# A decode step on one core: the residual stream stored tile by tile, each after its last addition, in place of one store at the end

## The reference

```python
def swiglu(h, w_gu, w_down):
    gu = h @ w_gu
    return (jax.nn.silu(gu[..., :D_FF]) * gu[..., D_FF:]) @ w_down
...
        x = x + jnp.concatenate([mix, mem_o], axis=-1) @ prm['w_out'][l]
        x = x + swiglu(rmsnorm(x, prm['g_ffn'][l]), prm['w_gu'][l], prm['w_down'][l])
...
    s_win = jnp.concatenate([cache_win_kv, rows_s[2]], axis=1)[:, -wb:]
```

## Time and profile before

| what | value |
| --- | --- |
| median of 3 timed executions | 3421.77 us |
| lowest and highest of them | 3414.11 and 3422.32 us |
| the profiled execution's own time | 3419.85 us |
| span of its trace, from the first to the last instruction | 3418.1 us |
| mean granted TensorE clock over the span | 0.937 of full speed |

### The profile page before, as it was taken

How to read it: one execution, slowest core, us unless ns; L and a number is a source line. 1 busy time by engine, 2 the same in 40 slices (tenths; PEclk the granted TensorE clock), 3 DMA queues, 4 the chain that set the end, 5 groups by cost and what they waited for, 6 DMA issues and landing times.

```text
span 3418.1 us, 49546 instructions
## 1 busy us (share of the span) xinstructions
PE 3093.7 (91%) x20055; PEld 2893.8 (85%) x20055; DVE 1262.7 (37%) x1969; ACT 980.7 (29%) x1658; POOL 344.3 (10%) x342
## 2 busy tenths in 40 slices
PE   6997958899999999998789689888689999999998
PEld 5997928799999999997679467777369999999998
DVE  5112751533322323341031477776143332332331
ACT  4212412423211111130431666655032321111110
POOL 0000130001000101000000234443000010000010
PEclk9998969899999999998799789999789999999999
DMA  4110042011111111112210000000411111111113
GB/s 149 58 44 13 1 131 73 32 37 47 45 50 43 47 47 48 40 52 77 90 59 29 3 1 1 2 1 23 127 75 44 43 43 50 44 48 50 45 43 123
DMA packets 63143, 169.11 MB, mean 49 GB/s; under 512 B 7334, under 2 KB 27923, under 8 KB 61859
## 3 DMA queue, kind: packets, MB, share of 16 engines
q1 hardware_dynamic: 50204, 151.00, 13.6%
q10 hardware_dynamic: 12776, 15.85, 1.4%
HBM read 153.02 MB, written 17.99 MB: 50 GB/s over the span
## 4 chain that ended last, share of the span: by engine, by line
PE 69%; DVE 6%; issue 4%; ACT 3%; DVEq 2%; SPq 2%; DMA 1%; POOL 0%; POOLq 0%; ACTq 0%
PE ps L347 57%; PE ps L2297 1%; PE ps L2254 1%; PE ps L2241 1%; PE ps L1789 1%; PE ps L1382 1%; PE ps L2243 1%; PE ps L1146 1%; PE ps L508 1%; SPq L1761 1%; SPq L1760 1%; DVE jf L2408 0%; PE ps L1349 0%; DVEq L2163 0%; PE ps L1375 0%
## 5 line engine op out<-in xcount | busy, mean ns | idle before, releaser
L347 PE MATMUL ps<-h_hi,w_hi 128*128 128x344 f32 x3360 | 725.0, 325 | 50.0 <-DVE h_lo L406 11.8
L347 PE MATMUL ps<-h_lo,w_hi 128*128 128x344 f32 x3360 | 718.5, 322 | 0.0
L347 PE MATMUL ps<-h_hi,w_lo 128*128 128x344 f32 x3360 | 714.9, 321 | 0.0
L347 PEld LDWEIGHTS ps<-h_hi,w_hi 128*128 128x128 f32 x3360 | 572.4, 190 | 56.0 <-issue 44.2
L347 PEld LDWEIGHTS ps<-h_lo,w_hi 128*128 128x128 f32 x3360 | 574.5, 191 | 0.0
L347 PEld LDWEIGHTS ps<-h_hi,w_lo 128*128 128x128 f32 x3360 | 565.1, 189 | 0.0
L299 DVE TENSOR_TENSOR w_lo<-w_raw,w_hi 128x1024 fp32r<-128x1024 f32 (+1 forms) x202 | 303.4, 1502 | 296.9 <-ACT w_hi L293 296.8
L293 ACT ACTIVATE w_hi<-w_raw 128x1024 fp32r<-128x1024 f32 (+1 forms) x202 | 208.6, 1034 | 520.5 <-PE ps L347 454.3
L1582 POOL TENSOR_TENSOR f_silu<-f_silu,nb_r 128x1032 f32<-128x1032 f32 x44 | 107.3, 2439 | 1758.1 <-ACT f_silu L1546 1758.1
L1504 DVE TENSOR_TENSOR xT<-xT,ps 128x1032 f32 (+1 forms) x64 | 78.7, 1229 | 448.3 <-PE ps L347 448.3
L347 PE MATMUL ps<-hid_hi,w_hi 128*128 128x344 f32 x1056 | 224.0, 320 | 0.0
(11 more groups left out here) (494 smaller groups left out, 3720.6 us busy)
## 6 DMA issues: line engine op xcount, KB each, us to landing
w_raw<-w_gu SPq DMA_DIRECT2D x88, 512.0 KB, 3.5
w_raw<-w_dn SPq DMA_DIRECT2D x32, 448.0 KB, 3.3
w_raw<-w_a SPq DMA_DIRECT2D x27, 512.0 KB, 3.5
w_raw<-w_o SPq DMA_DIRECT2D x16, 512.0 KB, 3.5
w_raw<-w_dn SPq DMA_DIRECT2D x16, 512.0 KB, 3.5
pages<-cmp SPq DMA_DIRECT2D x64, 128.0 KB, 2.5
w_raw<-w_b SPq DMA_DIRECT2D x9, 512.0 KB, 3.5
xT<-xT SPq DMA_DIRECT2D x1, 4128.0 KB, 17.0
```

Source lines behind the costliest of these rows:

```text
L347: mm = pe.matmul(ps[:, 3 * slot + c, 0:cut], w[:, slot, k * P:(k + 1) * P], a[:, k, c * cut:(c + 1) * cut], start=(k == 0 and w is w_hi an ...
```

## The change

In place of one store behind fence 18 there are eight stores, each behind the addition of its own tile. They stand in SyncE's program where the one store stood, behind the last load of weights and the copy into `o_win`. SyncE no longer waits for fence 18; the last wait is for all nine transfers.

```diff
         sw_o = sem("sw_o")
+
+        def store_y(sp):
+            T0 = segs["dn12"][0]
+            for i in range(KC):
+                sp.wait_ge(tile_free, T0 + i + 1)
+                sp.dma_start(O["o_y"][:, i, :], xT[:, i, :]).then_inc(sw_o, 16)
+
         block = ctx.enter_context(nc.Block())
...
             sp.dma_start(O["o_win"], A["win"].rearrange("b r c -> b (r c)")).then_inc(sw_o, 16)
-            sp.wait_ge(fence_s, 3 * 18)
-            sp.dma_start(O["o_y"], xT[:, :, :]).then_inc(sw_o, 16)
-            sp.wait_ge(sw_o, 32)
+            store_y(sp)
+            sp.wait_ge(sw_o, 16 * (1 + KC))
```

## The result

The changed kernel takes 3405.31 us (median of 6 executions, 3403.09 to 3410.06); over the same comparison the kernel before has 3415.1 us (median of 6, 3412.68 to 3422.32, the three known ones among them). The ratio is 0.9966, 95% interval 0.9954 to 0.9978: faster, by 7.5 to 15.7 us. Two further measurements of the same kernel gave 0.9968 (0.9956 to 0.998) and 0.9974 (0.9965 to 0.9983), the last one on another chip than the one before it.

The account below looks back on a forecast made before the run. PE, busy 91%, bounds the kernel and is untouched; the stake is the 11.7 us output tail. 11.2 − 2.7 = 8.5 us less gives 3413.3 off the median, 3411.4 off the profiled execution; predicted 3412.3, range 3405 to 3418.

Parts of the forecast that it names:

- landing of the last store: Last tile's 0.53 MB store, issue to landing: 2.7 us, bounds 2.0 and 5.3, in place of 11.2 for the whole.
- end of the addition to the end of the span: Program end: last addition over at 3406.43, span ending at 3409.6 in place of 3418.1.
- gain behind the last addition: At the program's end: 11.2 − 2.7 = 8.5 us less, bounds 9.3 and 5.5 us; chance 0.80 for 7.7 to 9.3.
- the wait for the fence: SyncE before the last store: waiting on the addition's own semaphore gains at most 0.07 us, counted as nothing.
- the seven other stores: Earlier tiles' stores behind the copy into o_win: all lie under PE's products and cost the path nothing.
- TensorE beside them: Products while stores read SBUF, 3369 to 3405: nothing counted, up to 0.4 us as bound; slowed PE has chance 0.02.
- About 0.3% (10.3 us) is what a measurement of this kernel can tell from no change: Whole-kernel measurement: expected gain, 0.25%, lies just inside this limit; 0.68 for within 0.3%, 0.28 for faster.
- a third of its 0.80: Whole kernel: chance 0.80 that the sum stands; about a third of it measured past 0.3% by scatter alone.
- theory 2: From the experiments: part of the gain is won ahead of the last addition; changed kernel's ratio 0.9966 or lower.
- theory 1: From the experiments: only the tail behind the last addition changes, 11.7 to 3.0 us, ratio 0.9975; the rest is scatter.
- slower last store: Rival at the last tile's store: small strided packets or idle-queue wake-up, 5.3 us, gain 5.9 us, 3414.9; chance 0.12.
- backlog: Rival in the DMA queue behind o_win: earlier stores delay the last; at 5.3 us a tile 11.5 us slower; chance 0.02.

Follow-up runs that it names:

- the two variants that have the same tail within 0.2 us: Changed kernel with two stores (tiles 0 to 6, then tile 7), 0.9977; changed kernel with tile 7's store cut in three, 0.9972; ratios to the kernel before.
- the moved copy: Changed kernel with the copy into o_win moved from ahead of the eight stores to behind them; ratio to the kernel before 1.0018.

## Why the prediction was wrong, and where it was right

The mechanism held in every step, and so did its sum. The conclusion drawn from the sum did not: I gave 0.68 to "within 0.3%", no change that can be told, and the kernel is faster, with an interval that ends at 0.9978.

| step | predicted | measured |
| --- | --- | --- |
| landing of the last store | 2.7 us, from 2.0 to 5.3 | 2.6 us in every trace with a whole tile, but 2.9 with a copy issued right behind it |
| end of the addition to the end of the span | 3.2 us (3406.43 to 3409.6) | 3.0 us |
| gain behind the last addition | 8.5 us, from 5.5 to 9.3 | 8.6 us |
| the wait for the fence | 0 to 0.07 us | 0.04 us (issue at 0.03 in place of 0.07) |
| the seven other stores | hidden | hidden; two stores do the same as eight |
| TensorE beside them | 0 to 0.4 us | 0: the eight additions span 69.3 us with and without the stores |

**What failed is the step "About 0.3% (10.3 us) is what a measurement of this kernel can tell from no change".** It took three executions 8.2 us apart as the measure of what can be told. The scatter of single executions is real, even larger than I thought (3408.5 to 3429.1 among 35 executions of the kernel before). But a comparison takes many executions of both, and the intervals of the ratios here reach 0.09 to 0.16% to either side, 0.12% in the median. The effect that the sum gave, 0.25%, is twice that, so it can be told from no change on either side of the 0.3% line. To put the 0.68 on "no change", and to name that the likeliest, was the mistake.

That the first ratio, 0.9966, also fell past the 0.3% line itself is scatter. The effect sat 1.8 us inside the line, as I had written, and the same kernel gave 0.9966, 0.9968 and 0.9974 where its tail explains 0.9975. The prediction had allowed a third of its 0.80 for that.

**The point, 3412.3, was 7.0 us too high.** 5.7 of them are its base: 3412.3 + 8.5 = 3420.8 stood for the kernel before, made from three timed executions and the profiled one, and six executions put it at 3415.1. The other 1.3 are the gain, 9.8 us between the two medians where the sum had 8.5. The measured time stands at the low end of the range, 0.3 us inside it.

**What the tail does not explain.** 8.6 us are a ratio of 0.9975. The three measurements of the changed kernel have a mean of 0.9969; with the two variants that have the same tail within 0.2 us (0.9977, 0.9972) it is 0.9971, 9.8 us. The difference of about 1 us is inside every one of the intervals, the third measurement came out at 0.9974, and theory 2's mark (a last addition at a fixed, earlier place) was absent. A deviation of 1 us also comes with no edit: the kernel before against itself gave 0.9997. I take theory 1 as shown for the 8.6 us; whether anything but scatter is behind the last 1 us stays open.

**One estimate of the prediction mixed two sources.** The 8.0 us that it draws from the fit in the Trainium skill ("DMA: Bandwidth & Descriptors", section "Anatomy of one DMA — SWDGE (gpsimd) path") takes the fit's 3.2 us for a tile from the trace's 11.2 us for the whole. The fit's own two figures, 11.7 and 3.2, differ by 8.5. The forecast did not use it, and the trace has 2.6 us for a tile on SyncE's queue.

**The rivals.** The slower last store fell with 2.6 us. The backlog did occur ahead of the end, as traffic behind the copy (tile 5's store took 5.9 us from issue to landing, and the longest of the earlier ones 18.5), and was over by about 3384, 14 us ahead of the last store. The prediction had 3393.6, which is 3385.4 in this trace with its shift of 8.2 us; the copy ahead of the stores landed in 15.6 us where the earlier trace rows had 17.9. In the DMA view of 3377 to 3387, by slices of 0.25 us:

```profile
GB/s 446 446 380 413 413 429 380 462 396 413 446 347 479 330 462 363 429 380 314 264 182 182 149 132 83 83 50 82 0 0 0 0 0 0 0 0 0 0 0 0
...
o_y<-xT SPq DMA_DIRECT2D x1, 516.0 KB, 5.9
```

The queue runs nearly full to 3381.5, thins out, and is empty from 3384 on, so nothing of it reached the end. What the backlog rival needed, work still to be done in the queue behind the last addition, is what the moved copy made, and that did turn the gain into a loss.

## What to carry to other kernels

Cutting up a store at the end of a program can win its transfer time less that of its last piece. Cut off the part that is ready earlier, once, with enough time ahead of the end for it to land; more stores of the same data gave nothing here. Only cutting the last tile's own work, products and addition included, gave 1.5 us more, and that is read from traces alone. The order in the queue matters more than the number of stores: a large transfer that does not depend on the last result goes ahead of them, as the copy behind them cost its full length. And before an effect of a quarter per cent is called not measurable, weigh it against the interval of a comparison of many executions, not against the distance between single ones; two profiles alone would have told 16.8 us where 8.6 were due.

## What the runs showed that was not expected

- One sum fits the store from SyncE's queue at four sizes, when no other transfer is in the queue: 1.4 us fixed, and the bytes at 430 GB/s. Measured were 1.8 us for 0.18 MB, 2.6 for 0.53, 10.0 for 3.70 and 11.2 for 4.23.
- The copy of 4.19 MB from memory to memory does not always take the same time. With nothing behind it, it landed in 17.9 us, but also in 14.7, 16.0 and 18.0 us in three further traces (the kernel before again, the store without the fence, the two stores). With stores queued behind it it took 15.1 to 15.7 us in six traces, and 15.7 at the end of the program. So the stores are not seen to slow it, and the 17.9 us that the prediction reckoned with came from a single trace.
- The issue of a single store can take far longer than the usual 0.35 us. The eight stores in the changed kernel (shortest, median, longest issue in ns, and landings in us):

```profile
L2766 SPq DMA_DIRECT2D o_y<-xT x8: 332/382/1245, 3360.8 to 3398.3; - x8
...
DMA to landing us min/median/max: 2.6/14.9/18.5
```

The long one is the fourth store of the burst behind the copy, tile 3. It took 1.25, 1.63 and 1.29 us in the three traces of the changed kernel and 1.79 where the last tile's products go by thirds, but 0.69 without the last store and 0.47 with the last store in thirds. With no copy ahead of the stores the third and the fourth took 1.34 and 1.38. It cost nothing there: in the changed kernel it ends at 3363.7, and the next store's addition is done only at 3368.6.
- An addition of 128x344 elements takes 0.51 us where 128x1032 take 1.23: 0.36 for a third more. An estimate from these two is 0.15 us that do not shrink with the size.
